# Moving five modulation chunks of layer 1 from the first output projection to behind the first expert loop

## The reference, cut to what matters

```
m = silu(c) @ w_mod[l] + b_mod[l]          # 6 * 1024 columns for each of two token groups
h = norm(x) * (1 + scale) + shift          # rows 0 and 1 of m: before the mixer
x = norm(ALPHA * x + gate * y)             # row 2: after the output projection
h2 = x * (1 + scale2) + shift2             # rows 3 and 4: before the experts
x = norm(ALPHA * x + gate2 * moe(h2))      # row 5
```

## Time and profile before

| what | value |
|---|---|
| median of 3 runs | 1915.07 us (1911.06 to 1917.36) |
| the profiled execution | 1911.47 us, its span 1909.6 us |
| PE busy | 1608.9 us, 84% of the span |
| DVE, ACT, POOL busy | 34%, 25%, 15% |
| moved by DMA | 278.66 MB, mean 146 GB/s |
| granted PE clock, mean over the span | 0.913 of full speed |

### The profile page before, as it was taken

How to read it: one execution, slowest core, us unless ns; L and a number is a source line. 1 busy time by engine, 2 the same in 40 slices (tenths; PEclk the granted TensorE clock), 3 DMA queues, 4 the chain that set the end, 5 groups by cost and what they waited for, 6 DMA issues and landing times. The chain is left out here.

```text
span 1909.6 us, 19915 instructions
## 1 busy us (share of the span) xinstructions
PE 1608.9 (84%) x7254; PEld 1003.4 (53%) x7263; DVE 642.3 (34%) x1263; ACT 467.9 (25%) x1031; POOL 287.8 (15%) x358
## 2 busy tenths in 40 slices
PE   3899998999899898995999917998999986999950
PEld 0464786566488785353444403336887463444420
DVE  0101366326444455643111134123443562111107
ACT  1311110122354441121111104115555011111111
POOL 1000110000154332121111033000000121111024
PEclk9999887999999998986999967997999976999985
DMA  9223400341110014255899756441002061999943
GB/s 298 89 89 104 172 1 0 105 142 65 43 45 23 1 45 175 90 185 211 297 335 336 273 124 218 151 157 64 1 1 96 15 225 62 326 333 334 340 165 97
DMA packets 127171, 278.66 MB, mean 146 GB/s; under 512 B 19232, under 2 KB 21492, under 8 KB 126956
## 3 DMA queue, kind: packets, MB, share of 16 engines
q1 hardware_dynamic: 110508, 217.96, 32.5%
q0 software_dynamic: 15328, 55.35, 9.0%
q10 hardware_dynamic: 1248, 4.19, 0.6%
HBM read 244.64 MB, written 32.84 MB: 145 GB/s over the span
## 5 line engine op out<-in xcount | busy, mean ns | idle before, releaser
L2519 PE MATMUL PS<-SLOTS,Z 128*128 128x512 f32 x576 | 260.0, 605 | 26.2 <-DMA SLOTS<-in_w_down 22.0
L2519 PEld LDWEIGHTS PS<-SLOTS,Z 128*128 128x128 f32 x576 | 108.5, 193 | 157.8 <-issue 155.1
L2109 PE MATMUL PS<-HT,SLOTS 128*128 128x320 f32 x640 | 174.7, 434 | 0.0
L2109 PEld LDWEIGHTS PS<-HT,SLOTS 128*128 128x128 f32 x640 | 120.9, 190 | 51.8 <-issue 2.6
L2450 PE MATMUL PS<-SLOTS,HT 128*128 128x512 f32 x320 | 141.4, 600 | 1.5 <-ACT HT L1452 1.5
L2538 PE MATMUL PS<-SLOTS,Z 128*128 128x512 f32 x288 | 130.1, 594 | 4.4 <-DVE Z L1914 4.4
L2119 PE MATMUL PS<-SLOTS,HT 128*128 128x512 f32 x240 | 110.0, 617 | 3.8 <-issue 3.8
L1910 DVE TENSOR_TENSOR Z<-Z,PS 128x256 f32<-128x256 f32 x36 | 15.2, 421 | 281.6 <-ACT Z L1335 281.6
L2593 PE MATMUL PS<-SLOTS,HT 128*128 128x512 f32 x240 | 108.4, 607 | 0.0
L2450 PEld LDWEIGHTS PS<-SLOTS,HT 128*128 128x128 f32 x320 | 60.6, 192 | 75.1 <-issue 73.3
L2538 PEld LDWEIGHTS PS<-SLOTS,Z 128*128 128x128 f32 x288 | 52.2, 191 | 57.4 <-issue 54.1
(11 more groups left out here) (395 smaller groups left out, 2416.4 us busy)
## 6 DMA issues: line engine op xcount, KB each, us to landing
SLOTS<-in_w_mod SPq DMA_DIRECT2D x24, 2048.0 KB
SLOTS<-in_w_gate SPq DMA_DIRECT2D x36, 1024.0 KB
SLOTS<-in_w_up SPq DMA_DIRECT2D x36, 1024.0 KB
SLOTS<-in_w_down SPq DMA_DIRECT2D x36, 1024.0 KB
expert_rows<-Z SPq DMA_DIRECT2D x36, 512.0 KB, 12.5
SLOTS<-in_w_in_even SPq DMA_DIRECT2D x8, 2048.0 KB
SLOTS<-in_w_qkv_odd SPq DMA_DIRECT2D x3, 2048.0 KB
h_rows<-Z POOLq DMA_DIRECT2D x10, 512.0 KB, 7.5
```

The lines of the kernel that those rows point to most:

```text
L2109: i = pe.matmul(b[:, 0:320], w[:, k, m * P:(m + 1) * P], HT[:, k, 320 * h:320 * h + 320], start=(k == 0), stop=(k == KT - 1))
L2519: x = pe.matmul(PS[:, 2 + u, :].rearrange("p (m c) -> p m c", m=2), XGT[:, u, k, :], w[:, :, k, :], start=(k == 0), stop=(k == KT - 1))
```

## The change

The five chunks move from "out0" to "moe". SP therefore loads them behind the first expert loop, before it waits for the gathers, and the third expert's weights now go into slot 2 while the output projection runs.

```
@@ modulation_parts
-    sizes = {"first": 4, "qa": 1, "ka": 1, "va": 1, "oa": 1, "vd": 1, "kd": 1, "qd": 1, "zb": 1, "out0": 5,
-             "moe": 0, "qkv2": 3, "qkv0": 2, "qkv1": 2}
+    sizes = {"first": 4, "qa": 1, "ka": 1, "va": 1, "oa": 1, "vd": 1, "kd": 1, "qd": 1, "zb": 1, "out0": 0,
+             "moe": 5, "qkv2": 3, "qkv0": 2, "qkv1": 2}
@@ load
-                elif item == ("mod",) + mod_parts["out0"][0]:
-                    sp.wait_ge(yb_var, TILES)
@@ sync_moe
-                if l == 0:
-                    sp.wait_ge(unit_done, unit_no[("modS",) + mod_parts["out0"][-1]] + 1)
...
-                for u in range(3):
+                if l == 0:
+                    sp.wait_ge(yb_var, TILES)
+                    load_expert(2, slice(2, 3))
+                for u in range(2 + l):
                     sp.wait_ge(unit_done, unit_no[last_unit(item_of[last_in_slot(n0 + u)])] + 1)
...
             sync_moe(0)
+            after_moe = loads.index(("moe", 0)) + 1
+            for item in loads[after_moe:after_moe + len(mod_parts["moe"])]:
+                load(item)
             for t in range(TILES):
                 sp.wait_ge(yg_gathered[t], 32)
             load_router(1)
-            for item in loads[loads.index(("moe", 0)) + 1:-1]:
+            for item in loads[after_moe + len(mod_parts["moe"]):-1]:
                 load(item)
```

## The result

| | before | after |
|---|---|---|
| median of 9 runs | 1914.97 us (1910.65 to 1917.82) | 1923.82 us (1918.00 to 1931.51) |
| the profiled execution, its span | 1911.47, 1909.6 us | 1925.31, 1923.5 us |
| granted PE clock, mean | 0.913 | 0.903 |

The ratio is 1.0053, with a 95% interval of 1.0036 to 1.0069: the change makes the kernel slower, by about 9 us.

A forecast was written before the change was run, and what follows sets the result against it. PE was taken to bound the first output projection, and a gather-to-layer-norm chain the stretch behind the expert loop, where PE idles. -19.7 + 30.5 = +10.8 us gives 1922.3 (execution) or 1925.9 (median); forecast 1924.0 us, range 1908 to 1932.

The forecast's parts named there:

- The projection, -19.7: First output projection: without the chunks PE takes 14.5 us per tile, not 18.8; everything after starts 19.7 us earlier.
- The third expert's load, 0: During the output projection: the early load was hidden under the routing and stays hidden, 0 us.
- The loop, 0: First expert loop: it keeps its slots, loads and order, 0 us.
- The landing of the fifth chunk: Behind the loop: gathers (22.1 us) and chunk loads (27.2 us) share the DMA engines; with 1 us for start and landing, 1163.4.
- From there to ACT, 7.6 us: From the last chunk's arrival to ACT's last copy: 7.6 us, with PE's clock at 1.2 GHz.
- The end of the gathers, 44 us after the first: Behind the loop: gathers, at half the DMA engines, end near 1157, 14 us before ACT is free.
- The gain, +30.5: Layer norm behind the loop: DVE multiplies by the gain at 1172.3 instead of 1141.77, 30.5 us later.
- The sum, +10.8 for the execution: Whole execution: -19.7 in the projection and +30.5 behind the loop give +10.8 us, 1922.3 from 1911.5.
- adding gathers leave the engines room: Rival, behind the loop: loads fill time adding gathers spend waiting; landing 1147.4, net -5.2 us, about 1908; chance 0.15.
- Loads that pass untouched: Rival, behind the loop: gathers do not slow the loads; landing 1141.3, net -11.3 us, about 1902; chance 0.09.
- Mixing at 331 GB/s: Rival, behind the loop: mixed traffic moves at the expert loop's rate; net +15.3, up to +20, 1928 to 1934; chance 0.10.
- A shortened projection that gives nothing: Rival, output projection: it does not get shorter because DVE or POOL ends it; net up to +30 us; chance 0.02.

The follow-up runs named there:

- E5: Changed kernel with the third expert's weights loaded last of the three again, behind the first two; 1923.83 us, ratio 1.0049 to the kernel before.
- E2: Changed kernel with the five chunk loads issued behind the ten gathers instead of beside them; 1929.01 us, ratio 1.0090 to the kernel before.
- E1: Changed kernel with ACT scaling the layer norm's rows between the five chunks instead of behind them; 1909.51 us, ratio 0.9982 to the kernel before.
- E7: Changed kernel with E1's ACT order and four chunks behind the loop, the fifth moved to the attention stretch; 1906.06 us, ratio 0.9955 to the kernel before.
- E8: E7 with the second layer's router weights loaded behind the attention's third weights; 1898.58 us, ratio 0.9921 to the kernel before.
- E4: Changed kernel with the second expert's rows gathered as plain copies instead of adding ones; 1915.68 us, ratio 1.0007 to the kernel before.

## Why the prediction was right

It forecast 1924.0 us, and 1923.82 was measured. The mechanism was the one forecast, and its terms were near, too. That the time agrees to 0.2 us is luck: the terms are off by 0.2 to 2.6 us, and the nine executions lie between 1918.00 and 1931.51.

- **The projection, -19.7:** measured -21.3. The tile takes 14.2 us, not 14.5. Most of the 1.6 us more is a thing that the step left out: with a chunk between them the two halves of a product took 7.03 + 7.13 = 14.16 us, in one piece they take 13.90, in each of five tiles. DVE did not become the bound.
- **The third expert's load, 0:** E5 shows 0.
- **The loop, 0:** 224.8 against 222.3 us in the two profiles, inside the scatter of the others.
- **The landing of the fifth chunk, 50.3 us after the first gather:** measured 1147.08 - 1096.54 = 50.5. Errors cancel in it. It counted 22.1 us for the gathers and 28.2 for the loads; in E2, where they run one behind the other, SP issues the loads 24.5 us after the first gather (1113.72 - 1089.23), and the fifth chunk's product comes 31.0 us after that. Both parts were counted too short, by 2.4 and 2.8 us, and side by side 4.9 us of these 55.4 are given back, most of them the hand-over.
- **From there to ACT, 7.6 us:** measured 1153.63 - 1147.08 = 6.6. The clock was back at 1.00 by then (1146 to 1148), the partial product took 1.92 us and not the 3.59 assumed.
- **The end of the gathers, 44 us after the first:** this was wrong. Of line L1000, the ten gathers, the last is issued at 1111.86, and the view of the line says:

```profile
DMA to landing us min/median/max: 4.8/11.1/16.2
```

  So all have landed by about 1128, some 32 us after the first: 22.1 us of the engines' time in 32 is more than half. No term of the sum hangs on it, but the layer norm's data waited some 25 us for ACT and not 14, and that is what E1 could win back.
- **The gain, +30.5:** measured 58.4 - 28.7 = +29.8. E1 shows that the step named the right place: 26.3 of it hang on ACT's order, the rest on the gathers' later landing.
- **The sum, +10.8 for the execution:** the two spans differ by 13.9 us, of which 2.1 lie ahead of the projection and 2.6 in the loop; the medians differ by 8.9.

The rivals fall as follows. That adding gathers leave the engines room: the part of it that can be true is at most E2's 4.9 us, where that rival needed about 16 to land the chunk 34 us after the first gather. The Trainium skill, page "DMA: Bandwidth & Descriptors", section "Two DMAs through the same engine are not ordered", says that within one queue of one engine descriptors start in order but are pipelined, and that the engine's read and write sides are separate queues. The gathers and the loads are issued by two engines, POOL and SP, and no run here looks into a single queue; what the runs show is about 1.5 us of busy time saved side by side. Loads that pass untouched: no, the fifth chunk came at 50.5 us, not at 28. Mixing at 331 GB/s: no, that would have been 54.8 us. A shortened projection that gives nothing: no, the stretch fell by 21.3 us. Two small slips decide nothing: by its own sum the prediction breaks even when the last chunk lands at 1141.77 + 19.7 - 8.9 = 1152.6 and not at 1147, and ACT has 14 copies for the five chunks, not 13.

What the prediction did not look at is how cheaply the loss could be avoided. It called the layer norm's place behind ACT's copies the cause, but took it as given with the move.

## What to carry to other kernels

Before moving work into an engine's idle time, list the instructions that the move puts ahead of others on the engines that serve it: here PE had room, and the 26 us were lost on ACT, for which the statistics of two tiles were ready 25 us before its turn came. When the chain is shortened, look at once for what is queued next: behind ACT's order stood a weight slot, and behind the slot six small loads on SP. Let a wait for late data stand behind work whose data are there.

## What the runs showed of the hardware

- *A short wait of PE cost more than itself.* In E7 PE waited 5.32 us at 1157; its next 16 records then took 3.64 us and a product 9.31, where in E8, without the wait, the same took 1.92 and 7.13. From the first attention product to the chunk at 1258.75 (1249.15 in E8) E7 took 9.9 us longer: 5.3 of them are the wait, 1.7 and 2.2 the slower records and the slower product. The windows from 1160 to 1168 (third column from the right, E7 first) show the granted clock at its lower level (1.2 GHz) for most of it in E7, behind PE's wait, and at the upper (2.4 GHz) in E8:

```profile
1160.00:1168.00 8.00, 5.54 (x26) 1.72 (x27) 0.00 (x0) 0.80 (x2) 0.00 (x0) 0.55 0.30 98
```

```profile
1160.00:1168.00 8.00, 8.00 (x22) 2.93 (x24) 0.41 (x2) 1.57 (x5) 0.00 (x0) 1.00 0.79 271
```

  The other 2.4 us by which E7's attention stretch is longer were not followed up.
- *Adding gathers are dear where DMA is full.* Beside the loads the stretch with them moves 255 GB/s at a share of 1.05; with plain copies in their place (E4) it is 398 at 1.04.
- *Small loads hold a queue.* The router's four inner loads take SP 2.5 us to issue when the engines are free, in the kernel before, and 9.4 to 10.9 us behind full loads; while the last of them move, at 1148 to 1152 in E1, it is 13 GB/s at a share of 0.34.
